# Two landing places and four split places in the weight ring of a six-layer fp32 kernel

## The chip, the cores and the metric

The kernel runs on one NeuronCore of a Trainium2 chip. The metric is the device time of one execution in microseconds (us), as the median of several runs. TensorE is called PE, VectorE DVE, ScalarE ACT, GpSimd POOL; SyncE (SP) issues nearly all DMAs.

## The reference, cut to what matters

A sequence of 256 tokens with 1024 channels goes through two blocks, everything in fp32. The first block has an RWKV-7 layer and a sparse attention layer (DSA), each with a SwiGLU layer behind it, and all four are modulated by vectors made from a condition `c`. The second has four residual layers: FoX attention, GLA, gated delta net (GDN), FoX attention.

```python
mod = silu(c) @ ada_w[i] + ada_b[i]            # 1024 x 6144, twice: one vector times a matrix
hin = x * (1 + sc1) + sh1
y = rwkv7(hin) or dsa_attention(hin)
x = layernorm(ALPHA * x + (1 + gt1) * y)
hin = x * (1 + sc2) + sh2
x = layernorm(ALPHA * x + (1 + gt2) * ((silu(gate) * up) @ ffn_w_out))
...
for layer in range(4):                         # fox, gla, gdn, fox
    x = x + mixer(rms_norm(x))                 # each: @ w_in, the mixer, @ w_out
```

Every weight matrix is used once, so some 240 MB of weights are streamed from HBM in one execution.

## The kernel before, in words

**Chunks.** `plan` cuts every weight matrix into chunks: KG = 4 row blocks of 128 rows by up to 512 columns, 1 MB when full. All chunks of the program stand in one list in the order in which they are used, numbered by `g`. There are 224: 48 *direct* ones, which belong to `ada_w`, and 176 others.

**Landing ring.** `w_raw` has NRAW places. Chunk `g` lands in place `g % NRAW`. SP issues the DMAs in the order of the list, and before it issues chunk `g` it waits until chunk `g - NRAW` has been consumed. A direct chunk is consumed when PE has multiplied it (L294, `Ada.pe_sums`: the condition vector times the chunk; an item is two chunks). Any other chunk is consumed when ACT has written its rounded part `w_hi` (L188, `split_hi`) and DVE has written the rest `w_lo` (L197, `split_lo`).

```python
if c["g"] >= NRAW:
    old = self.chunks[c["g"] - NRAW]
    sp.wait_ge(self.direct if old["direct"] else self.lo_done, old["idx"] + 1)
```

**Split ring.** `w_hi` and `w_lo` have NSPL places each. ACT and DVE wait with chunk `idx` until PE has used chunk `idx - NSPL`. PE makes an fp32 product of three passes, x_hi w_hi, x_hi w_lo and x_lo w_hi (L220 to L222, `mm_block`): 24 matmuls for a full chunk and 256 tokens.

**Stages.** The program is a row of stages; at each boundary all engines meet. A projection stage (`stage_project`, `stage_ffn_in`, `stage_rwkv_in`) runs over column blocks of two chunks each, and on each engine everything stands in one written order. `stage_project` writes it like this for ACT and for DVE:

```python
for m, c in enumerate(chunks):
    while due and c["idx"] - NSPL >= job[due[0]][-1]["idx"]:
        take(due.pop(0))
    if m >= done:
        split(c)
```

`take(n)` copies the finished block `n` out of PSUM and then does the side work of that block (`fox_sides`, `gla_sides`, `gdn_sides`, `bias_sides`). So with NSPL = 3 block `n` is taken after the split of chunk `2n+3` and before that of `2n+4`. In the FoX projection one piece of side work is `lf` on DVE (L2153, side work of block 2), and PE has two small matmuls that read it (L2159) behind its block 2, which is chunks 4 and 5.

**Start of a projection.** The activations are normalised, turned by PE (L535) and split too (`act_lead`, `dve_lead`). For the three projections behind a layernorm (both `ffn_in` and `dsa_in`) an `ada` item is put in there: PE multiplies it (L294), ACT copies it out (L312), PE turns it into a column (L302). ACT's order there is `split(0)`, then the `ada` copy, then the normalisation (`xn`, L517), and then the activations' high parts. PE's order is the item, ten filler matmuls (`keep_warm`, L204), the turn L302, four more fillers, the transposes L535.

**Ada elsewhere.** Items stand in `stage_begin` (four), `rwkv_lora` (two), `rwkv_prepare` (two), in `rwkv_mid` (six between pairs of small matmuls, L1287 and L1311, and two at the end), in `dsa_prepare` (one), `dsa_select` (three), `dsa_attend` (one).

Of the kernel before, what the change touches and what calls it, by code (L numbers as in the profile page):

```python
# [17 lines left out]
KD = D // P  # L18
COLS = 512
KG = 4  # L20
NRAW = 3
NSPL = 3
F = 2816
NEG = -1.0e30

# [47 lines left out]
class Core:  # L73

    def __init__(self, nc, a, ctx):
# [12 lines left out]
        self.modc = self.fixed("modc", [P, 2, 6 * KD])  # L89
        self.raw = self.fixed("w_raw", [P, NRAW, KG, COLS])  # L90
        self.s0 = self.at
        top = end // 32 * 32
        size = NSPL * KG * COLS * 4
        self.lo_at, self.hi_at = top - size, top - 2 * size
# [4 lines left out]
        self.ps = ctx.enter_context(nc.psum_tensor("ps", [P, 8, COLS], F32))  # L99
        self.wsem = [ctx.enter_context(nc.semaphore(f"w_landed{i}")) for i in range(NRAW)]  # L100
        self.hi_done = ctx.enter_context(nc.semaphore("w_hi_done"))
# [22 lines left out]
    def split_rings(self):  # L124
        return (self.place("w_hi", [P, NSPL, KG, COLS], self.hi_at, F32R),
                self.place("w_lo", [P, NSPL, KG, COLS], self.lo_at, F32R))

# [11 lines left out]
    def plan(self, name, w, blocks, direct=False):  # L139
# [3 lines left out]
        for cols in blocks:  # L143
# [3 lines left out]
            for k0 in range(0, ktot, KG):  # L147
                nk = min(KG, ktot - k0)
                g = len(self.chunks)
                kind = sum(c["direct"] == direct for c in self.chunks)  # L150
                self.chunks.append(dict(g=g, slot=g % NRAW, direct=direct, idx=kind, k0=k0, nk=nk,
                                        width=width, w=w, cols=cols))
# [8 lines left out]
    def issue(self, sp, upto):  # L161

        upto = min(upto, len(self.chunks))
        while self.issued < upto:
            c = self.chunks[self.issued]
# [3 lines that stand above are left out]
# [9 lines left out]
    def issue_mod(self, sp, items):  # L178
        l, b = items[-1]
        self.issue(sp, self.mod[l, b][-1]["g"] + 1 + NRAW)  # L180

    def split_hi(self, act, hi, c):

        s = c["idx"] % NSPL
        act.wait_ge(self.wsem[c["slot"]], self.landed(c))
        if c["idx"] >= NSPL:
            act.wait_ge(self.used, c["idx"] - NSPL + 1)  # L187
        self.nc.scalar.copy(hi[:, s, 0:c["nk"], 0:c["width"]],  # L188
# [3197 lines left out]
```

## Time and profile before

| what | value |
|---|---|
| median of 3 runs | 1651.54 us (1649.9 to 1652.76) |
| the profiled execution: its own time | 1648.74 us |
| the profiled execution: span of its instructions | 1647.0 us |
| PE busy | 1488.5 us, 90% of the span |
| DVE busy | 872.5 us, 53% |
| ACT busy | 670.2 us, 41% |
| DMA from the SP queue, share of 16 engines | 46.6% |
| mean DMA rate | 148 GB/s |

Busy time is the union of an engine's instructions. The instructions are in the order of the program, so the place of a row tells its stage: the begin stage ends at 39 us, `rwkv_mid` runs from 179 to 310, the three projections behind a layernorm start at 343, 563 and 755, the two FoX projections at 985 and 1487.

### The profile page before, as it was taken

The page shows a single profiled execution, that of the slowest core. Times are in us where ns is not written, and L with a number is a line of the kernel's source. Part 1 is how long each engine was busy: PE and PEld are TensorE (multiplying, and loading weights), DVE is VectorE, ACT ScalarE, POOL GpSimd, SP SyncE.
Part 4 walks back from the last instruction along what each step waited for, and adds up shares of the span by engine and source line. Part 5 has one row for each costly group of instructions (what it writes and reads, how often), then busy time and mean ns, then how long its engine had stood idle before and what let it go on. Part 6 is the DMA issues. An engine that isn't in the chain of part 4 may idle for free. (4 is left out here: it accounts for less than half of the span.)

```text
span 1647.0 us, 19055 instructions
## 1 busy us (share of the span) xinstructions
PE 1488.5 (90%) x7546; PEld 1171.5 (71%) x7546; DVE 872.5 (53%) x1161; ACT 670.2 (41%) x917; POOL 199.3 (12%) x109
## 2 busy tenths in 40 slices
PE   6999899989999998888999989978998985878987
PEld 2774669758877675565887868966886875767976
DVE  0756683764535454356554445745435587465644
ACT  1533432334333235343443316544452675235542
POOL 0005440130000110303000000300000032300300
PEclk8999899999999998899999989999999997899999
DMA  8655380546545564424653528814533531027821
GB/s 313 215 171 151 129 307 1 191 143 202 181 128 192 165 218 144 146 86 144 205 180 127 204 94 183 211 51 138 177 100 93 180 114 53 1 77 161 206 94 52
DMA packets 156852, 244.11 MB, mean 148 GB/s; under 512 B 14022, under 2 KB 95898, under 8 KB 156252
## 3 DMA queue, kind: packets, MB, share of 16 engines
q1 hardware_dynamic: 155612, 237.56, 46.6%
q0 software_dynamic: 1152, 5.34, 0.9%
q8 instruction: 60, 0.98, 0.3%
q14 instruction: 28, 0.23, 0.0%
HBM read 241.77 MB, written 1.11 MB: 147 GB/s over the span
## 5 line engine op out<-in xcount | busy, mean ns | idle before, releaser
L197 DVE TENSOR_TENSOR w_lo<-w_raw,w_hi 128x2048 fp32r<-128x2048 f32 (+3 forms) x176 | 393.0, 2240 | 291.8 <-ACT w_hi L188 291.6
L220 PE MATMUL ps<-w_hi,act_hi 128*128 128x512 f32 (+4 forms) x1216 | 470.4, 387 | 20.9 <-DVE act_lo L568 8.3
L188 ACT CAST w_hi<-w_raw 128x2048 fp32r<-128x2048 f32 (+3 forms) x176 | 316.2, 1802 | 380.0 <-PE ps L222 212.1
L222 PE MATMUL ps<-w_hi,act_lo 128*128 128x512 f32 (+4 forms) x1216 | 463.5, 381 | 0.0
L221 PE MATMUL ps<-w_lo,act_hi 128*128 128x512 f32 (+4 forms) x1216 | 463.1, 381 | 0.0
L220 PEld LDWEIGHTS ps<-w_hi,act_hi 128*128 128x128 f32 x1216 | 230.7, 190 | 68.3 <-DVE act_lo L568 12.0
L221 PEld LDWEIGHTS ps<-w_lo,act_hi 128*128 128x128 f32 x1216 | 230.6, 190 | 36.8 <-issue 1.2
L222 PEld LDWEIGHTS ps<-w_hi,act_lo 128*128 128x128 f32 x1216 | 230.5, 190 | 36.9
L204 PE MATMUL ps<-con 128*128 128x512 f32 x208 | 102.9, 640 | 24.3 <-DVE up L3165 18.0
L204 PEld LDWEIGHTS ps<-con 128*128 128x128 f32 x208 | 41.1, 209 | 70.7 <-issue 70.7
L294 PE MATMUL ps<-w_raw,condz 128*32 128x512 f32 x384 | 61.8, 748 | 23.7 <-DMA w_raw<-in_ada_w 13.7
L698 ACT ACTIVATE proj<-ps,nstat 128x456 f32<-128x456 f32 (+2 forms) x64 | 37.2, 632 | 105.3 <-PE ps L222 105.3
L220 PE MATMUL ps<-w_hi,ffn_gh 128*128 128x512 f32 x176 | 70.0, 398 | 0.0
L221 PE MATMUL ps<-w_lo,ffn_gh 128*128 128x512 f32 x176 | 69.6, 395 | 0.0
L222 PE MATMUL ps<-w_hi,ffn_gl 128*128 128x512 f32 x176 | 69.6, 395 | 0.0
L465 POOL TENSOR_TENSOR nstat<-nstat,con 128x2 f32<-128x2 f32 x7 | 4.9, 698 | 498.6 <-DVE nstat L487 299.4
L839 ACT ACTIVATE ffn_s<-ps 128x256 f32<-128x256 f32 x44 | 14.5, 381 | 93.8 <-PE ps L222 93.8
L294 PEld LDWEIGHTS ps<-w_raw,condz 128*32 128x32 f32 x384 | 10.4, 120 | 50.2 <-issue 25.8
L864 DVE TENSOR_TENSOR ffn_h<-ffn_s,ps 128x256 f32<-128x256 f32 x44 | 16.6, 418 | 53.4 <-PE ps L817 45.0
L302 PEld LDWEIGHTS ps<-con,ada_part 128*128 128x128 f32 x192 | 29.6, 234 | 21.3 <-issue 17.3
L312 ACT COPY ada_part<-ps 128x512 f32<-128x512 f32 x24 | 14.0, 583 | 66.7 <-PE ps L294 66.7
L220 PEld LDWEIGHTS ps<-w_hi,ffn_gh 128*128 128x128 f32 x176 | 33.1, 188 | 9.0 <-DVE w_lo L197 1.2
(479 smaller groups left out, 1834.5 us busy)
## 6 DMA issues: line engine op xcount, KB each, us to landing
w_raw<-in_ada_w SPq DMA_DIRECT2D x48, 1024.0 KB, 6.3
w_raw<-in_ffn_w_in SPq DMA_DIRECT2D x88, 512.0 KB, 4.9
w_raw<-in_fox_w_in SPq DMA_DIRECT2D x32, 912.0 KB, 8.8
w_raw<-in_ffn_w_out SPq DMA_DIRECT2D x20, 1024.0 KB, 5.1
w_raw<-in_rwkv_w_rkv SPq DMA_DIRECT2D x12, 1024.0 KB, 6.3
w_raw<-in_gla_w_in SPq DMA_DIRECT2D x10, 896.0 KB, 4.7
w_raw<-in_gdn_w_in SPq DMA_DIRECT2D x10, 896.0 KB, 4.9
w_raw<-in_fox_w_out SPq DMA_DIRECT2D x8, 1024.0 KB, 5.0
```

Source lines behind the costliest of these rows:

```text
L188: self.nc.scalar.copy(hi[:, s, 0:c["nk"], 0:c["width"]], self.raw[:, c["slot"], 0:c["nk"], 0:c["width"]]).then_inc(self.hi_done, 1)
L197: self.nc.vector.tensor_tensor(lo[:, s, 0:c["nk"], 0:c["width"]], self.raw[:, c["slot"], 0:c["nk"], 0:c["width"]], hi[:, s, 0:c["nk"], 0:c ...
L204: self.nc.tensor.matmul(self.ps[:, bank, :], self.c("ident"), moving, start=True, stop=True)
L220: nc.tensor.matmul(out(t)[:, 0:w], xh[:, k, tok], hi[:, s, j, 0:w], start=first, stop=False)
L221: nc.tensor.matmul(out(t)[:, 0:w], xh[:, k, tok], lo[:, s, j, 0:w], start=False, stop=False)
L222: r = nc.tensor.matmul(out(t)[:, 0:w], xl[:, k, tok], hi[:, s, j, 0:w], start=False, stop=last)
L294: r = core.nc.tensor.matmul(self.sums[32 * j:32 * j + 32, :], core.condz[:, k, :], core.raw[:, c["slot"], j, :], start=(k < KG), stop=(k > ...
L302: r = core.nc.tensor.matmul(self.turned[:, 4 * n + j:4 * n + j + 1], self.part[n % 2][:, j * P:j * P + P], core.c("ones")[:, 0:1], start=T ...
L312: core.nc.scalar.copy(self.part[n % 2][:, :], self.sums).then_inc(sem("ada_part"), 1)
L698: core.nc.scalar.activation(dst(n, t), out(t), ACT.Copy, scale=scale).then_inc(sem("taken"), 1)
L839: nc.scalar.activation(act_s[:, n % 2, t, :], ps[:, 2 * (n % 2) + t, 0:T], ACT.Silu).then_inc(sem("silu"), 1)
L864: nc.vector.tensor_tensor(h_s[:, n % 2, t, :], act_s[:, n % 2, t, :], ps[:, 2 * (n % 2) + t, T:2 * T], ALU.mult).then_inc(sem("h"), 1)
```

## The change

The landing ring gets two places in place of three, the split rings four places each in place of three. Nothing else is edited; but both constants are also used in the written orders: SP looks NRAW chunks ahead at the end of a stage, and `stage_project` and `stage_rwkv_in` place the taking of a block by NSPL. A place is 8 KB of each partition, and there are two split rings, so the rings grow from 72 to 80 KB and the scratch space between them shrinks by 8 KB.

```diff
 COLS = 512
 KG = 4
-NRAW = 3
-NSPL = 3
+NRAW = 2
+NSPL = 4
 F = 2816
```

## Rows read from the trace of the kernel before

**Rows 1.** Page, its head.
```profile
span 1647.0 us, 19055 instructions
```
**Rows 2.** Tile w_raw: durations ns min/median/max, and who waited for its users.
```profile
L188 ACT CAST w_hi<-w_raw x176: 862/1900/1943, 47.0 to 1624.9; 128x2048 fp32r<-128x2048 f32 x106, 128x1824 fp32r<-128x1824 f32 x36, 128x1792 fp32r<-128x1792 f32 x24, 128x1024 fp32r<-128x1024 f32 x4
L197 DVE TENSOR_TENSOR w_lo<-w_raw,w_hi x176: 992/2286/4490, 48.9 to 1626.9; 128x2048 fp32r<-128x2048 f32 x106, 128x1824 fp32r<-128x1824 f32 x36, 128x1792 fp32r<-128x1792 f32 x24, 128x1024 fp32r<-128x1024 f32 x4
...
  PEld ps L220: 1.2, 2
```
**Rows 3.** Waits of PE: who, for whom, us in total, times, longest.
```profile
PE ps L294 <- DMA w_raw<-in_ada_w: 13.7, 9, 3.8
PE ps L2691 <- ACT acc L2679: 12.3, 4, 4.7
```
**Rows 4.** Windows, eight chunks of the RWKV projection, users of w_hi: length, busy, clock, DMA.
```profile
57.90:101.42 43.52, 39.42 (x129) 24.03 (x128) 17.37 (x8) 15.29 (x8) 1.00 0.66 228
```
**Rows 5.** DMA issues at 208.16 and 209.01: count, KB, us to landing.
```profile
w_raw<-in_ada_w SPq DMA_DIRECT2D x1, 1024.0 KB, 5.2
...
w_raw<-in_ada_w SPq DMA_DIRECT2D x1, 1024.0 KB, 7.0
```
**Rows 6.** Timeline of ACT, GDN projection, casts ahead of a wait of PE.
```profile
1354.96 2.94 ACT L188 CAST w_hi<-w_raw 128x1600 fp32r<-128x1600 f32 x2
```
**Rows 7.** Timeline of PE, begin stage, its last ada chunk.
```profile
29.99 1.93 PE L294 MATMUL ps<-w_raw,condz 128*32 128x512 f32 x8 [0.67 <-DMA w_raw<-in_ada_w]
```
**Rows 8.** Timeline of PE, rwkv_prepare, its last ada chunk.
```profile
176.27 1.07 PE L294 MATMUL ps<-w_raw,condz 128*32 128x512 f32 x8 [0.75 <-DMA w_raw<-in_ada_w]
```
**Rows 9.** Timeline of PE, rwkv_mid: second, sixth and last ada item.
```profile
213.39 1.06 PE L294 MATMUL ps<-w_raw,condz 128*32 128x512 f32 x8 [0.44 <-DMA w_raw<-in_ada_w]
...
236.59 1.92 PE L294 MATMUL ps<-w_raw,condz 128*32 128x512 f32 x16
...
305.06 1.06 PE L294 MATMUL ps<-w_raw,condz 128*32 128x512 f32 x8 [1.77 <-DMA w_raw<-in_ada_w]
```
**Rows 10.** Timeline of PE, dsa_select, its last ada item.
```profile
659.90 3.69 PE L294 MATMUL ps<-w_raw,condz 128*32 128x512 f32 x16
```
**Rows 11.** DMA issues at 344.7, 564.7 and 756.9.
```profile
w_raw<-in_ffn_w_in SPq DMA_DIRECT2D x1, 512.0 KB, 7.9
...
w_raw<-in_dsa_w_in SPq DMA_DIRECT2D x1, 1024.0 KB, 7.0
...
w_raw<-in_ffn_w_in SPq DMA_DIRECT2D x1, 512.0 KB, 7.6
```
**Rows 12.** Timeline of ACT, then of PE, start of the first ffn_in.
```profile
343.14 1.90 ACT L188 CAST w_hi<-w_raw 128x2048 fp32r<-128x2048 f32 x1 [13.23 <-PEq L236]
345.79 0.58 ACT L312 COPY ada_part<-ps 128x512 f32<-128x512 f32 x1 [0.76 <-PE ps L294]
...
351.01 0.95 PE L302 MATMUL ps<-con,ada_part 128*128 128x1 f32 x8
...
353.62 1.91 PE L535 MATMUL ps<-con,xn 128*128 128x128 f32 x16
```
**Rows 13.** DMA issues at 988.6, 992.2 and 1010.8: FoX chunks 3, 4 and 8.
```profile
w_raw<-in_fox_w_in SPq DMA_DIRECT2D x1, 912.0 KB, 5.4
...
w_raw<-in_fox_w_in SPq DMA_DIRECT2D x1, 912.0 KB, 9.1
...
w_raw<-in_fox_w_in SPq DMA_DIRECT2D x1, 912.0 KB, 8.4
```
**Rows 14.** Timeline of DVE, then of PE, first FoX projection.
```profile
1016.52 4.03 DVE L197 TENSOR_TENSOR w_lo<-w_raw,w_hi 128x1824 fp32r<-128x1824 f32 x2 [5.00 <-ACT w_hi L188]
1020.47 0.17 DVE L2153 TENSOR_TENSOR lf<-tmp 128x16 f32<-128x16 f32 x1
...
1020.79 0.60 PE L2159 MATMUL ps<-ntri,lf 128*8 128x256 f32 x2
```
**Rows 15.** Windows, behind a wait of PE of 18 us that ends at 1405.8.
```profile
1405.80:1409.20 3.40, 3.40 (x4) 1.46 (x5) 3.37 (x2) 0.00 (x0) 0.00 (x0) 0.51 0.00 0
```

## The prediction, made before the changed kernel was run

> **What bounds the kernel now.** I read the head of the page, then the waits of PE, then everything that touches w_raw, then the timelines where the two views pointed. PE is busy for 90% of a span of 1647.0 us [rows 1]. It never waits for a landed or a split weight in a projection: the only such wait in 176 chunks is 1.2 us, of the weight load [rows 2]. Where it does wait for landings is the ada work, nine times, 13.7 us in all [rows 3]. So the reader is to see two uses of one landing ring. In projections it has slack: eight chunks take PE 43.5 us, 5.44 each, at full clock [rows 4], while a place is free again after landing (5.2 us alone [rows 5]), cast 1.9 and subtraction 2.3 [rows 2], 9.4 us; three places give a chunk each 3.1 us, two give one each 4.7 us. In ada work PE eats a chunk in 1.1 us, and only what has landed ahead hides a landing.
>
> **What the edit moves.** (a) SP issues a chunk when the chunk two before is consumed, no longer three before. (b) ACT and DVE may split four chunks ahead. (c) In the written order, take(n) and its side work move behind the split of chunk 2n+4. (d) The addresses of the scratch tiles shift; no row prices that, I put it at 0 (a large effect would have to be in every stage alike).
>
> **Fourth split place: what it can bring.** PE's wait for splits is 1.2 us, so (b) alone can give back at most that. By (c) casts run before side work instead of after it. PE waits for ACT four times in the GDN projection, 12.3 us [rows 3]; ahead of one of them ACT has two casts of 2.94 us together [rows 6], of which one can now be done earlier, half of it: -1.3 with the subtraction it frees. The other three have no cast in front. I take -1.3; the ends are 0 and -13.5.
>
> **Ordinary projections.** 4.7 us for a chunk against PE's 5.44, and four split chunks as a cushion: cost 0. The cover is 0.75 us a chunk; it is gone when landings take over 6.6 us.
>
> **Ada streams.** Two chunks issued 0.86 us apart land after 5.2 and 7.0 us, so at 213.3 and 216.0, 2.7 apart [rows 5]; in a queue each further chunk costs 2.7, and the latency of an empty queue shows in full at 5.1 to 5.2.
> Begin: the chunks 2 to 7 are each issued one consumption later. Chunk 6 goes out behind x, lands at 29.7, and chunk 7, issued when 5 is eaten at 26.2, lands 2.7 behind it at 32.4; before, PE began it at 29.99 [rows 7]. +2.4.
> rwkv_prepare: its two items are four chunks. The third is issued at 171.1 and lands 176.2, the fourth 2.7 later, where PE began at 176.27 [rows 8]. +2.7.
> rwkv_mid: the pair at 207.0 has landed early in both kernels. The next pair is issued at 208.2 and 209.0 and lands at 213.3 and 216.0: its second chunk is done at 217.1, not at 214.45 (213.39 + 1.06 [rows 9]). From there each first chunk lands 5.1 us behind the end of the first one before it, each second chunk 5.1 behind the second before it but at least 2.7 behind its partner, and PE has 4.0 us of small matmuls between: pairs end at 217.1, 223.4, 231.1, 237.4, 245.1. The last of these ended at 238.5 [rows 9]: +6.6, and PE is what the stage goes by here, its next step is fixed filler. At the end two items stand in a row: third chunk issued when the first is eaten, lands 5.1 later, the fourth 2.7 behind: begin of the last at 314.35 in place of 305.06 + 6.6 [rows 9], +2.7. DVE's last work ended 0.6 us behind PE's before, which hides 0.6 of it. +8.7 for the stage.
> dsa_select: six chunks, two landed ahead instead of three. Chunks 3 to 6 land at 656.2, 658.9, 663.2, 666.0; the last item ended at 659.90 + 3.69 = 663.6 [rows 10], now at 668.0. The topk on DVE is done by then and filler follows on PE. +4.4.
> rwkv_lora, dsa_prepare, dsa_attend: at most two chunks are wanted before a pause longer than 8 us. 0. Together 18.2. Bounds: 9 (every chunk beyond the first late one hidden by a clock that is at half level anyway), 25.
>
> **Start of the three projections behind a layernorm.** This is the wait that I look for first, because it blocks something else. The list has ada, ada, chunk 0. With three places chunk 0 is issued when the last chunk of the stage before is split, long ahead. With two, both places hold the ada chunks, and chunk 0 is issued when PE has eaten the first, at 344.2, 564.7 and 756.3, behind the loads of the layernorm's gains. The chunks issued at these moments before landed at 352.6, 571.7 and 764.3 [rows 11] (their second halves, issued 0.4 to 0.6 later). ACT begins its stage with split(0), where it stood at 343.14 [rows 12]: it now stands idle until 352.6, casts 1.9, copies the ada part 0.6 [rows 12], and PE turns it at 355.1 instead of 351.01. Behind the turn come fillers and the transposes 2.6 us after it, at 357.8, where they stood at 353.62 [rows 12]: +4.2. Queued behind ACT's cast is also the normalisation, which PE's transposes need; it is done at 357.4, just in time. The same sum for the others gives +3.8 (transposes at 573.20 before) and +5.5 (764.09 before). Together 13.5. Bounds: 5, if PE's idle fillers could be passed; 17, if POOL's work on x, which moves too, slows more of DVE's.
>
> **The two FoX projections.** Here landings are slower: 5.4 us for chunk 3, 9.1 for chunk 4, 8.4 for chunk 8 [rows 13], each issued with at most one other chunk still on its way. Chunks 2, 4, 6, 8 share one place. A chunk is cast in 1.7 (1.9 scaled to 456 columns) and subtracted in 2.0 [rows 14], with handovers 3.85. So: 2 is issued when chunk 0 is split, 988.6, lands 994.0; 4 is issued 997.9, lands 1007.0; 6 is issued 1010.9, lands 1016.1 (5.2 taken); 8 is issued 1020.0, lands 1028.4, split at 1032.3. PE is hardly late yet (chunk 5 is split at 1016.7, needed at 1015.7). But lf stood on DVE right behind the split of chunk 7 and was ready at 1020.6, just as PE came to use it at 1020.79 [rows 14]. By (c) it now stands behind the split of chunk 8: ready at 1032.4. PE waits in front of L2159: +11.7. While it waits, the ring fills, so the later slow chunks cost nothing more. The second FoX layer has the same pattern 501.8 us on: together +23.4. Lower bound: all landings 5.4, then 8 is split at 1025.8, +5.2 each. Upper bound: 14 each, with the slow chunks afterwards uncovered. After a wait of 18 us PE ran 3.4 us at a granted clock of 0.51 [rows 15], that is at the level of 1.2 GHz, half its work lost: 1.7 for each of these two waits, 3.4.
>
> The Trainium skill bears on (a). "Trainium Kernel Development and Optimization", Best Practices, says "Double-buffer for performance: Overlap DMA with compute". That a second buffer is enough would make (a) free, and the sum would be -1.3; the trace agrees for the ordinary projections (4.7 against 5.44) and speaks against it wherever something else than a steady stream waits. [...]
>
> **The sum.** 18.2 + 13.5 + 23.4 + 3.4 - 1.3 = 57.2 us. The profiled execution took 1648.74 (span 1647.0, 1.7 around it), 2.8 below the median, so I add to the median: 1651.5 + 57.2 = 1709.
>
> **Rivals.**
> 1. FoX landings were slow only through company, and two places make each 5.4. For it: 5.4 for chunk 3. Against: chunk 8 had none. Waits of 5.2 each and no lost clock: 1651.5 + 18.2 + 13.5 + 10.4 - 1.3 = 1692.
> 2. The starts are covered: chunk 0 lands early enough, or fillers absorb the delay. For it: SP's queue is short there. Against: fillers are in order, nothing can pass them. 57.2 - 13.5: 1695.
> 3. Landings overlap more often than I think and take 7.0 us [rows 5] everywhere: a place turns in 11.3, a chunk each 5.65 against 5.44. 0.2 for some 140 chunks, 29 more: 1738. Against: one chunk in flight, while the other is split.
> 4. Two landing places are enough, as the skill's rule has it, and PE finds its work: -1.3 to 0, 1650 to 1652. This is also the case that the edit does nothing. Against: ada work waits even with three.
> 5. Faster: side work with ACT and DVE no longer behind casts. All four waits in GDN and the 1.2 go, -13.5: 1638. It decides if the landing terms stay under 13.5 in sum. For it: 12.3 us in rows 3. Against: three of the four waits have no cast in front.
>
> **Numbers.** Forecast 0.57, rival 1 0.13, rival 2 0.10, rival 3 0.12, rival 4 0.05, rival 5 0.03. The range 1685 to 1730 takes in the forecast with its bounds and rivals 1 and 2, and leaves out 0.2. A measurement of this kernel can tell 0.2%, 3.3 us, from no change. Faster 0.03, within it 0.05, slower 0.92.
>
> **What would show it.** In the profile after: PE's waits for w_raw<-in_ada_w near 30 us instead of 13.7; L188 at the start of both ffn_in and of dsa_in waiting for a DMA, with L535 behind it 4 to 5.5 us late; in front of L2159 a wait of some 10 us for DVE's L2153, twice, with L197 before it waiting for a cast that waits for in_fox_w_in; and in ffn_out, gla_in and the plain projections no wait for w_lo. It would be wrong if chunks were issued earlier than the list says, if FoX landings shrink, or if a wait in the steady stream shows up at L220.

## The result: 79.5 us slower, 4.9%

The changed kernel takes 1730.2 us (median of 4 runs, 1725.1 to 1740.2), the kernel before 1650.7 (4 runs, 1647.3 to 1652.8); the ratio is 1.0491, 95% interval 1.0434 to 1.0549. Run once more beside other kernels it gave 1734.0 (6 runs, 1724.9 to 1743.3) and a ratio of 1.0500 (1.0466 to 1.0534). The prediction was 1709, range 1685 to 1730: the direction is right, the loss is 1.4 times the forecast one, 79.5 us for 57.2, and the time just outside the range. The execution profiled took 1734.73 us, 86.0 above that of before, so the readings below add up to 86.0.

The page of the changed kernel, its head and the row of the granted clock in 40 slices of the span (9 is 90% or more of full speed):

```profile
span 1733.0 us, 19054 instructions
PEclk9999779898999999799999999899999997989999
```

The two 7s side by side are the slices from 173 to 260 us, rwkv_prepare and rwkv_mid. The waits of PE, in us, times and longest, as in [rows 3]:

```profile
PE ps L294 <- DMA w_raw<-in_ada_w: 33.6, 21, 4.5
PE ps L2159 <- DVE lf L2153: 22.8, 2, 11.6
PE ps L302 <- ACT ada_part L312: 13.3, 5, 5.0
PE ps L2691 <- ACT acc L2679: 10.9, 4, 3.5
PE ps L220 <- DVE w_lo L197: 0.6, 1, 0.6
```

Against [rows 3] the waits for ada landings have grown from 13.7 to 33.6 us, there is a wait for lf of 11.6 and one about as long, and the turn of the ada sums now waits for ScalarE. The steady stream is as it was: one wait of 0.6 us for a split weight, and in this window over the RWKV projection, all of PE's instructions counted and not only the users of w_hi as in [rows 4], PE is busy from end to end at full clock (in the kernel before it is 43.52 of 43.52 us too):

```profile
57.90:101.42 43.52, 43.52 (x194) 36.05 (x193) 28.88 (x28) 22.71 (x19) 0.00 (x0) 1.00 0.66 233
```

I laid the two traces side by side, chunk by chunk, and took by how much later PE begins each chunk. What each stretch adds, with the forecast behind it:

| stretch | added, us | forecast |
|---|---|---|
| begin | 3.5 | 2.4 |
| rwkv_prepare | 4.5 | 2.7 |
| rwkv_mid | 25.6 | 8.7 |
| dsa_select and its neighbours | 4.7 | 4.4 |
| starts of ffn_in0, dsa_in, ffn_in1 | 7.0, 4.7, 7.0 | 4.2, 3.8, 5.5 |
| FoX projections | 14.4, 14.5 | 13.4 each (11.7 wait, 1.7 clock) |
| GDN and all the rest | 0.1 | -1.3 |
| sum | 86.0 | 57.2 |

So one row is off by 17 us and the others by 3 at most. (The 0.1 is a sum of small terms of both signs, +1.3 in the first ffn_out and -0.7 from GDN to the next FoX layer among them.) The row that is off, rwkv_mid, in the profile, as windows that hold the same work of PE: from the first ada item of rwkv_mid to the sixth, and from there to the next item. Columns: window, its length, busy us and instructions of PE, PEld, DVE, ACT and POOL, granted clock, DMA share, GB/s. First the kernel before:

```profile
207.00:238.51 31.51, 30.74 (x250) 18.88 (x249) 29.28 (x66) 11.52 (x21) 12.71 (x12) 1.00 0.94 329
238.51:298.79 60.28, 60.28 (x580) 56.18 (x580) 25.34 (x44) 13.51 (x22) 10.02 (x4) 1.00 0.11 38
```

Then the changed kernel, with a third window inside the first:

```profile
214.90:264.75 49.85, 41.64 (x250) 25.17 (x249) 31.37 (x67) 11.72 (x21) 14.85 (x13) 0.76 0.67 224
264.75:328.37 63.62, 63.62 (x582) 58.20 (x581) 22.12 (x42) 13.53 (x22) 7.32 (x3) 0.95 0.07 24
225.75:233.08 7.33, 7.33 (x32) 6.37 (x32) 6.81 (x16) 1.76 (x3) 1.34 (x2) 0.50 0.62 225
```

The same 250 matmuls keep PE busy for 41.64 us instead of 30.74. Of the 18.3 us that this window grew, 7.4 are idle time and 10.9 are slower work. The third window shows what kind: PE never stands in it, has no ada chunk in it, and runs at a granted clock of 0.50, the level of 1.2 GHz. About as many bytes come in over a longer time, at 224 GB/s for 329. The first two windows once more, now cut where the granted clock changes:

```profile
214.90:221.66 6.76, 5.33 (x45) 3.15 (x48) 6.14 (x19) 2.73 (x5) 1.30 (x2) 1.00 0.66 229
221.67:235.31 13.64, 12.65 (x60) 7.24 (x56) 12.64 (x30) 2.83 (x5) 3.44 (x3) 0.50 0.56 195
235.32:245.55 10.23, 6.90 (x57) 3.96 (x49) 9.62 (x19) 1.66 (x3) 2.65 (x3) 1.00 0.87 288
245.56:255.79 10.23, 10.23 (x48) 6.88 (x48) 2.94 (x2) 2.83 (x5) 1.27 (x2) 0.50 0.38 123
255.80:266.03 10.23, 7.77 (x64) 5.21 (x61) 0.00 (x0) 2.25 (x4) 7.45 (x4) 1.00 0.96 309
266.04:272.86 6.82, 6.82 (x19) 4.40 (x19) 0.00 (x0) 1.07 (x2) 2.76 (x1) 0.50 0.44 154
272.87:328.37 55.50, 55.50 (x553) 52.51 (x551) 22.12 (x42) 11.87 (x19) 3.26 (x2) 1.00 0.00 1
```

The level alternates with the items. PE stands in every second one (2.4, 3.3 and 2.5 us in all). Soon behind each of these waits the clock falls to half; while PE works at half clock the next two chunks land, so that the item between has no wait, and the clock comes back. In PE's timeline the first wait stands just before the window from 225.75 to 233.08, and the lines behind L1311 are later waits of the stage:

```profile
221.25 1.58 PE L294 MATMUL ps<-w_raw,condz 128*32 128x512 f32 x8 [1.43 <-DMA w_raw<-in_ada_w]
223.81 1.93 PE L294 MATMUL ps<-w_raw,condz 128*32 128x512 f32 x8 [0.99 <-DMA w_raw<-in_ada_w]
...
229.48 3.67 PE L1311 MATMUL ps<-v,kgram 128*128 128x64 f32 x16
...
244.46 1.06 PE L294 MATMUL ps<-w_raw,condz 128*32 128x512 f32 x8 [2.94 <-DMA w_raw<-in_ada_w]
...
334.81 1.93 PE L294 MATMUL ps<-w_raw,condz 128*32 128x512 f32 x8 [3.53 <-DMA w_raw<-in_ada_w]
337.52 1.93 PE L294 MATMUL ps<-w_raw,condz 128*32 128x512 f32 x8 [0.78 <-DMA w_raw<-in_ada_w]
```

PE stands 1.43 and 0.99 us; the ada chunk behind the second takes 1.93 us (1.06 in [rows 9]), and the matmuls of L1311 take 3.67 (2.00 in the kernel before). The start of ffn_in0, which answers to [rows 12], first ACT, then PE:

```profile
385.94 1.90 ACT L188 CAST w_hi<-w_raw 128x2048 fp32r<-128x2048 f32 x1 [22.20 <-DMA w_raw<-in_ffn_w_in]
387.74 0.58 ACT L312 COPY ada_part<-ps 128x512 f32<-128x512 f32 x1
...
388.38 1.87 PE L302 MATMUL ps<-con,ada_part 128*128 128x1 f32 x8 [5.02 <-ACT ada_part L312]
393.66 2.93 PE L535 MATMUL ps<-con,xn 128*128 128x128 f32 x16
```

ACT stands at its first cast for a landing, the copy of the ada sums queues behind it, PE waits 5.02 us, and then the turn (L302) and the transposes (L535) run at the lower clock, 1.87 and 2.93 us where [rows 12] have 0.95 and 1.91. And the first FoX projection, DVE and PE, for [rows 14]:

```profile
1089.25 2.06 DVE L197 TENSOR_TENSOR w_lo<-w_raw,w_hi 128x1824 fp32r<-128x1824 f32 x1 [4.42 <-ACT w_hi L188]
1091.23 0.17 DVE L2153 TENSOR_TENSOR lf<-tmp 128x16 f32<-128x16 f32 x1
...
1091.45 1.02 PE L2159 MATMUL ps<-ntri,lf 128*8 128x256 f32 x2 [11.58 <-DVE lf L2153]
```

This is the forecast chain: lf behind the split of a late chunk. PE began the projection 58.1 us late, and the forecast had lf ready at 1032.4 on the old scale, so at 1090.5; it was ready at 1091.4.

### The profile page after: what moved, and what is told of

Same layout as the page of the kernel before. It is cut to its first block and busy times, and to the rows that moved or that the text cites. A ratio compares the mean times of both kernels' runs of the same rounds, so it can differ in the third digit from the quotient of the medians.

```text
span 1733.0 us, 19054 instructions
## 1 busy us (share of the span) xinstructions
PE 1524.2 (88%) x7546; PEld 1189.1 (69%) x7546; DVE 867.7 (50%) x1161; ACT 669.8 (39%) x917; POOL 194.2 (11%) x109
## 5 line engine op out<-in xcount | busy, mean ns | idle before, releaser
L197 DVE TENSOR_TENSOR w_lo<-w_raw,w_hi 128x2048 fp32r<-128x2048 f32 (+3 forms) x176 | 386.7, 2208 | 294.9 <-ACT w_hi L188 294.8
L204 PE MATMUL ps<-con 128*128 128x512 f32 x208 | 113.8, 697 | 24.5 <-DVE up L3165 18.3
L294 PE MATMUL ps<-w_raw,condz 128*32 128x512 f32 x384 | 69.8, 832 | 42.4 <-DMA w_raw<-in_ada_w 33.6
L204 PEld LDWEIGHTS ps<-con 128*128 128x128 f32 x208 | 45.0, 229 | 75.5 <-issue 75.5
L839 ACT ACTIVATE ffn_s<-ps 128x256 f32<-128x256 f32 x44 | 14.5, 382 | 133.0 <-PE ps L222 133.0
L302 PEld LDWEIGHTS ps<-con,ada_part 128*128 128x128 f32 x192 | 35.4, 277 | 37.9 <-ACT ada_part L312 19.2
L302 PE MATMUL ps<-con,ada_part 128*128 128x1 f32 x192 | 36.7, 314 | 13.4 <-ACT ada_part L312 13.3
```

The costliest lines, as they stand in the source:

```text
L197: self.nc.vector.tensor_tensor(lo[:, s, 0:c["nk"], 0:c["width"]], self.raw[:, c["slot"], 0:c["nk"], 0:c["width"]], hi[:, s, 0:c["nk"], 0:c ...
L204: self.nc.tensor.matmul(self.ps[:, bank, :], self.c("ident"), moving, start=True, stop=True)
L294: r = core.nc.tensor.matmul(self.sums[32 * j:32 * j + 32, :], core.condz[:, k, :], core.raw[:, c["slot"], j, :], start=(k < KG), stop=(k > ...
L302: r = core.nc.tensor.matmul(self.turned[:, 4 * n + j:4 * n + j + 1], self.part[n % 2][:, j * P:j * P + P], core.c("ones")[:, 0:1], start=T ...
L839: nc.scalar.activation(act_s[:, n % 2, t, :], ps[:, 2 * (n % 2) + t, 0:T], ACT.Silu).then_inc(sem("silu"), 1)
```

## The experiments

"Ring" below is the ring of landing places. Every time stands beside the kernel before on the same chip (1649.4 to 1652.1); the ratio has its 95% interval.

**1. Landing places alone: three split places kept.**

```diff
-NRAW = 3
+NRAW = 2
```

> Two landing places, three split ones: the half of the change that takes away. Against the kernel before. Theory (landing place is the whole loss): the ada waits on PE stay near 33 us, the layernorm leads and rwkv_mid as in the changed kernel; in the FoX projections lf is cast one chunk earlier in the written order, so each of the two long waits (11.6 and 11.3 us) shrinks by 2 to 4 us; GDN's two casts wait again for a place (its wait about 4.7, not 3.3 us). Sum: within 8 us of the changed kernel's 1730, about 1725. Rival (the fourth split place and the order that goes with it make a large part of the loss): the FoX waits vanish, under 1710. Rival (the fourth place softens the loss): over 1738.

Measured: 1729.3, ratio 1.0481 (1.0446 to 1.0516). The landing place alone gives practically the whole loss in time. Its waits of PE for lf and for ACT in GDN:

```profile
PE ps L2691 <- ACT acc L2679: 12.3, 4, 4.7
PE ps L2159 <- DVE lf L2153: 8.2, 2, 4.6
```

GDN's wait is that of before, as expected. Each lf wait shrank by some 7 us, more than the 2 to 4 that I gave it. The FoX projections add 7.5 and 8.3 us, not 14.4 and 14.5. These 13 us less are in the profiled execution, which at 1719.95 us is the fastest of the four; the median is only 1 us below that of the changed kernel, so the medians don't show them.

**2. The changed kernel with the written order as for three split places.**

```diff
-                while due and c["idx"] - NSPL >= job[due[0]][-1]["idx"]:
+                while due and c["idx"] - 3 >= job[due[0]][-1]["idx"]:
```

(and the same in the written order of the RWKV projection)

> The changed kernel (2 landing, 4 split) with the written order of the evacuations and side work as it was for three split places. Theory as predicted (order alone makes the FoX wait, since lf was ready before): the two waits of PE for lf go from 11.6 and 11.3 us to 1 or less, 1705 us. Rival (lf waits for landings of chunks ahead of it in either order, the order adds only one chunk of it): the waits shrink to 7 to 9 us each, 1722 to 1726. In both cases the ada waits and GDN are unchanged.

Measured: 1726.1, ratio 1.0462 (1.0437 to 1.0486), PE's wait for ACT in GDN again 12.3 us, the two FoX projections +7.7 and +10.6. The theory (1705, waits of 1 us) is refuted and the rival has the time, but not its waits of 7 to 9 us: they are 7.7 us for both together. The order is some 4 to 7 us of each projection's 14, the landings are the rest. With the wait for lf shorter, PE comes to the late chunks sooner: it now waits 4.7 us for their split parts (`w_lo`), for 0.6 in the changed kernel. GDN's gain is gone although the fourth split place is there, so it takes the place and the order together.

**3. The order alone: the kernel before with the written order as for four** (the edit of experiment 2, with 4 in place of NSPL = 3).

> The kernel before (3 landing, 3 split) with the written order as it would be for four split places, and nothing else. Theory (the order costs only where a late landing stands ahead of it): with three landing places lf is 3 to 5 us later than PE wants it, twice: 1655 to 1660 us. Rival (order alone makes the 11 us waits): 1674. Rival (order costs nothing with three landing places): 1650.7, no different.

Measured: 1665.9, ratio 1.0104 (1.0081 to 1.0128), and these waits:

```profile
PE ps L2691 <- ACT acc L2679: 13.5, 4, 4.4
PE ps L2159 <- DVE lf L2153: 8.1, 2, 4.0
```

The lf waits are as expected, but the time is 6 us above the expected 1655 to 1660. With the lower clock behind them the projections add 6.4 and 7.0 us. Added to the 7.5 and 8.3 of the first run that is 13.9 and 15.3, near the 14.4 and 14.5 of both together. Of the rest, 3.1 us lie in GDN; of 5.9 us that the profiled execution is late before ffn_in0, 4.9 are gone again before FoX, and I can assign neither. In the times the halves don't add: 79.7 us for the landing place alone and 16.3 for the order alone are 96, for the 79.5 of both. So only the FoX terms can be added, and the order costs less where the landings are late already.

**4. Don't let PE stand for lf.** L2159 moves from behind block 2 to behind block 4 of the FoX projections, then to behind block 3, then to block 3 with the pool engine's second root ahead of the gate's transfers in its queue.

```diff
-    @on("pe", 2)
+    @on("pe", 4)
     def _(pe, sem):
         pe.wait_ge(sem("lf"), 1)
```

> The changed kernel with PE's two small matmuls on lf put behind block 4 of each FoX projection rather than behind block 2, so that PE doesn't stand still for lf; nothing else. If the long waits are the cost of FoX (11.6 and 11.3 us, and 1.2 us of lower clock behind each) and nothing else is late behind them: 25 us less than the changed kernel, 1705 us. Rival (PE stands still because chunks land too slowly and would wait for weights in its place): 2 to 8 us less, 1722 to 1728.

> The changed kernel with PE's matmuls on lf behind block 3 of each FoX projection (block 2 in the kernel, block 4 in the last such run, where PE then stood 5.8 us twice waiting for the normalized q and k that the pool engine makes behind ncum). Theory (what was saved at lf there was given back at the norm, since the pool's queue holds ncum ahead of the second norm): with one block less delay the wait for lf is 2 us or less and the norm's wait 0 to 2 us, so each projection gains 9 to 12 us and the time is 1708 to 1714. Rival (with two landing places PE waits for weights instead): 1722 or more.

> The changed kernel with PE's matmuls on lf behind block 3, and in the pool engine's queue the second reciprocal root (for the norm) ahead of the gate's transfers (ncum out and in) rather than behind them. Theory (FoX's loss is a chain of small steps whose order was tight for three landing places: lf first, then the norm): both the lf wait and the 5.4 us norm waits vanish and each FoX projection is 0 to 4 us longer than in the kernel before (14.4 us in the changed kernel): 22 to 27 us less than the changed kernel. Rival (two landing places hold the projection however the side work is ordered): 8 to 12 us less, as with the matmul moved alone.

Measured: 1733.5 (1.0503, 1.0465 to 1.0540), 1724.5 (1.0456, 1.0400 to 1.0513) and 1728.1 (1.0466, 1.0442 to 1.0491; the changed kernel beside it 1734.0). The gains that I expected, 25, 16 to 22 and 22 to 27 us, failed all three times; only in the second did the rival hold. Each wait for lf shrank to 1.2 us or less, and the projections still add 10 and 7 us in the third. There, first DVE and then PE:

```profile
1118.52 2.06 DVE L197 TENSOR_TENSOR w_lo<-w_raw,w_hi 128x1824 fp32r<-128x1824 f32 x1 [5.51 <-ACT w_hi L188]
1120.50 2.29 DVE L2218 TENSOR_TENSOR proj<-proj,st 128x2048 f32<-128x2048 f32 x1
...
1122.84 2.40 PE L2231 MATMUL ps<-con,proj 128*128 128x128 f32 x10 [4.01 <-DVE proj L2218]
```

It is the same picture one step on: the norm now stands behind a split that waits 5.51 us for a late chunk, and PE waits for the norm. The pool's queue was not the main cause: with it reordered PE still waits 6.5 us for the norm, 9.7 without, and the times of the two runs don't differ clearly. Every small step of this projection is written between splits, so with two landing places the whole chain of steps is late.

**5. The ada streams alone, with two landing places; everything else with three.** (A second line, not shown, makes SP stop one chunk earlier where the last chunk that it looks ahead to is an ada chunk.)

```diff
+            if c["direct"] and c["g"] >= 2:
+                old = self.chunks[c["g"] - 2]
+                sp.wait_ge(self.direct if old["direct"] else self.lo_done, old["idx"] + 1)
```

> The kernel before (3 landing, 3 split, its written order), but an ada chunk's transfer also waits until the chunk two before it is used, so that the ada streams alone run as with two landing places and the projections with three. Theory (the streams with an unsplit chunk on PE are where most of the loss is, through landing and then through the lower clock): PE's waits for ada landings 30 us or more, rwkv_mid 20 to 28 us longer, the sum over the five ada stages 32 to 45 us: 1683 to 1695 us. Forecast of the prediction for the same streams: 18.2 us, 1669. Rival (the loss in rwkv_mid comes from the projection's chunks or from the moved buffers): under 1660.

Measured: 1688.0, ratio 1.0229 (1.0197 to 1.0261), +38.6 us. The table above has 38.3 for these streams, the forecast 18.2. (The execution profiled here was the fastest of four, 34.9 us above that of before.) The waits are nearly those of the changed kernel:

```profile
PE ps L299 <- DMA w_raw<-in_ada_w: 34.4, 21, 4.4
```

**6. rwkv_mid alone with two landing places** (chunks 16 to 31 of the 48, held as in experiment 5), **and the same with extra matmuls** ahead of the second chunk of each item but the first; their results go nowhere.

```diff
         for c in core.mod[l, b]:
+            for _ in range(warm if c["k0"] else 0):
+                core.nc.tensor.matmul(core.ps[:, 7, 256:512], core.c("ident"), core.con[:, 0:256], start=True, stop=True)
             pe.wait_ge(core.wsem[c["slot"]], core.landed(c))
```

> The kernel before, with only the ada chunks used in rwkv_mid (16 of 48) held to two landing places; every other chunk has three. The prediction gave this stage +8.7 us; the profiles of the changed kernel show its end some 25 to 30 us later than before. Theory (the stage's stream alone loses 18 to 25 us): 1669 to 1675 us. Rival (the prediction's size was right and the rest comes from neighbouring stages): 1658 to 1661.

> The same, with six extra matmuls of 256 columns ahead of the second chunk of each ada item but the first in rwkv_mid, so that TensorE's granted clock stays up. Theory (about 10 us of this stage's loss is the halved clock on the small matmuls between the chunks): 6 to 10 us less than the run without them. Rival (the landings alone set the stage's pace, so the slower matmuls lie in time that would be waited anyway, or the extra matmuls cost what they give): within 3 us.

> As the run with six extra matmuls, with four (1.7 us at full clock). With six the granted clock stayed up, but PE then had work without a pause between the chunks (3.79 us from one chunk to the next and 4.97 to the item behind, 8.76 an item), so the filler itself set the pace and the stage was still 16 us longer than before. Four fit in the 1.6 to 1.7 us by which a chunk lands behind its partner. Theory (clock and landings share the loss, and the prediction's sum of +8.7 holds for a stream at full clock): 1659 to 1663 us, an item near 7.5 us. Rival (the clock falls again with less filler): 1672 or more.

> The same with two extra matmuls (0.87 us). Theory: the pauses that are left, near 0.8 us each, either leave the clock up, and the time is that of four extra matmuls or 1 us less, or they bring half clock back in part: 1665 to 1672. Without extra matmuls it was 1678.8.

Measured, with the stage's length from the first ada matmul to the end of the last one (before 99.1 us, from 207.0 to 306.1; changed kernel 124.6):

| extra matmuls | time | ratio (95%) | stage |
|---|---|---|---|
| none | 1678.8 | 1.0166 (1.0142 to 1.0191) | 125.6 |
| two | 1666.4 | 1.0094 (1.0065 to 1.0122) | 114.6 |
| four | 1663.8 | 1.0077 (1.0050 to 1.0104) | 112.7 |
| six | 1667.0 | 1.0100 (1.0076 to 1.0125) | 119.4 |

The stage's stream alone costs 28.5 us, more than the 19 to 25 expected. Giving PE more to do takes 12 to 15 us off the kernel's time, where 6 to 10 had been expected of six; four miss their 1659 to 1663 by 1 us, two are within theirs. Each stage length is of one execution: in the ten others that have two landing places here and no extra matmul it is 120.1 to 128.7 us, in the three others with six it is 117.6 to 119.7. Windows over the same work, none first, then four:

```profile
205.69:255.60 49.91, 42.30 (x250) 24.91 (x249) 31.54 (x67) 11.72 (x21) 15.07 (x13) 0.74 0.68 227
255.60:319.96 64.36, 64.36 (x582) 59.28 (x581) 22.13 (x42) 13.51 (x22) 7.01 (x3) 0.94 0.07 21
```

```profile
210.46:252.40 41.94, 40.47 (x290) 25.90 (x289) 31.57 (x67) 11.51 (x21) 14.60 (x12) 1.00 0.78 261
252.40:312.68 60.28, 60.28 (x580) 56.17 (x580) 22.14 (x42) 13.50 (x22) 7.93 (x4) 1.00 0.08 29
```

With 40 instructions more (20 matmuls, each recorded as two), PE is busy for less time, 40.47 us for 42.30, at a clock of 1.00 for 0.74. The second window has no extra matmul in it and still falls from 64.36 to 60.28, exactly the length it has before the change. Six are worse than four since they take more than the pause: an ada chunk follows its partner's start after 3.79 us with six, 2.92 with four. The first late item still has its pause with four, and the clock stays at 1.00 behind it:

```profile
216.85 1.06 PE L301 MATMUL ps<-w_raw,condz 128*32 128x512 f32 x8 [1.47 <-DMA w_raw<-in_ada_w]
```

**7. The extra matmuls (six) in the changed kernel,** run twice:

> The changed kernel, with six matmuls of 256 columns (about 2.6 us at full clock, their output unused) ahead of the second chunk of each ada item but the first in rwkv_mid. Theory (PE's waits pull the granted clock to half, and the small matmuls between the ada chunks then take 7.3 us instead of 4.0): the granted clock of rwkv_mid near 1.0, the pair's matmuls 1.06 us a chunk, the stage 8 to 14 us shorter although PE has more to do: 1717 to 1723 us. Rival (the clock is low for another reason, or the stage is held by landings alone): no shorter, 1730 to 1742.

> The changed kernel with the extra matmuls in rwkv_mid a second time. In its first run the ada matmuls of rwkv_mid all took 0.59 us (full clock) and the end of the stage came 26.4 us late, against 29 to 39 us for the six others, but the median of its times was not below the changed kernel's. Theory (the lower clock is worth 8 to 10 us in rwkv_mid): beside the changed kernel on the same chip 6 to 12 us less. Rival (the extra matmuls cost as much as the clock gives back): within 3 us of it.

Measured: 1734.0 (1.0501, 1.0466 to 1.0537) and 1732.6 (1.0486, 1.0464 to 1.0508), the latter beside the changed kernel's 1734.0. The clock came back and the stage fell to 117.6 and 119.7 us, but the medians hardly moved. The unaltered changed kernel, profiled once more beside the second, had a stage of 122.3, so that only 2.6 us of it are a gain over its neighbour. On these runs alone the rival stood; it is why experiment 6 was made.

**8. The first split behind the normalization,** in the changed kernel and in the kernel before.

```diff
-        split(0)
         if self.ada:
             self.ada.act_part(act, sem, 0)
         self.act_norm(act, sem)
+        split(0)
```

> The changed kernel with ScalarE's cast of the projection's first chunk put behind ada_part and the normalization in the lead of each projection with an ada item, so that the late landing of that chunk no longer holds ada_part. Theory of the prediction (leads +13.5 us because the cast stands ahead): the waits of the turn matmuls for ada_part fall from 13.3 us to 4 or less, ffn_in0, dsa_in and ffn_in1 each 4 to 7 us shorter: 1712 to 1718 us. Rival (the chunk is as late for the first block as it was for ada_part): the waits move to the first block's w_lo, 1726 to 1732.

> The kernel before with the cast of each projection's first chunk behind ada_part and the normalization in the lead. With three landing places that chunk has landed in time in most leads, so nothing is waited for there: within 3 us of 1650 us. Rival (some of the 7 to 11 us that the leads wait for the turn of the ada sums comes from this cast): 4 us or more faster.

Measured: 1718.0, ratio 1.0416 (1.0375 to 1.0456), some 12 us less than the changed kernel; in the kernel before 1651.5, ratio 0.9999 (0.9981 to 1.0017), no different. PE's waits for ada_part in front of the turn (L302) fall from 13.3 to 1.4 us; a part comes back as the first block's wait for its operand `act_lo` (L576), 11.7 us for 6.2. The starts of the three projections fall from 7.0, 4.7 and 7.0 to 3.4, -0.2 and 3.3 us.

**9. Both repairs together, then with six extra matmuls.**

> The changed kernel with both repairs of written order: first split behind the normalization, lf matmul behind block 3 with the second root ahead of the gate's transfers. Each alone gave about 13 us and 6 us. Theory (they lie at different places, so they add): 1711 to 1716 us, still 60 us above before, since the ada streams are untouched. Rival (the landing ring takes back at the next place what one repair saves): 1718 or more.

> The same with the extra matmuls in rwkv_mid. Theory of the clock: 6 to 10 us less than the run without them, 1703 to 1709. Rival: within 3 us of it.

Measured: 1709.5 (1.0354, 1.0327 to 1.0380) and 1704.1 (1.0321, 1.0297 to 1.0344). The repairs add up: 22.6 us by the ratios, 1 to 2 us more than expected. The extra matmuls gain 5.4 us here, at the edge of the expected 6 to 10. More than 50 us of the loss stay; no version was found that beats the kernel before.

## Why the prediction fell short, step by step

**What bounds the kernel; ordinary projections at 0.** Right: 0.6 us of waits for split weights in 176 chunks. Rival 3, landings of 7.0 everywhere, is near in time (1738), but the loss in the steady stream that makes it did not come.

**Ada streams, 18.2 us: this is the step that failed.** It measured 38.6 us alone (experiment 5). In the prediction's words, each second chunk lands "at least 2.7 behind its partner, and PE has 4.0 us of small matmuls between". The landings do come so: PE begins the two chunks at 221.25 and 223.81, as they land; the forecast's 213.3 and 216.0, with the 7.9 us by which the stage's first item is late, are 221.2 and 223.9. But the 4.0 us are a duration at full clock. PE now stands 2.4 to 3.3 us in every second item, the granted clock falls to 0.50 behind it, and the small matmuls take 7.3 us, the chunks 1.93 for 1.06. From 217.1 on the forecast let the pairs end 6.3, 7.7, 6.3 and 7.7 us after one another; they end 10.3, 9.4, 10.7 and 8.6 apart, and it is the pairs without a wait that are 4 us longer. The forecast even named half clock, as the reason for its lower bound, and priced it for the FoX waits only. The run with four extra matmuls divides the stage's 26.5 us (125.6 against 99.1): 12.9 are gone with the clock back up, and the 13.6 that stay are landings plus what the extra matmuls themselves take, for a forecast of 8.7. In the times it is 28.5 and 11.8 us. This divides single executions, and the stage differs by several us between executions (experiment 6). The same mechanism is a part of rwkv_prepare, whose last chunk took 1.93 us for the 1.07 of [rows 8].

"TensorE: Matmul & The Clock Gate" of the Trainium skill, section HAM oscillation — how this bites in real kernels, describes a loop in which waits for transfers between batches of matmuls bring the lower clock back each time. Its waits are longer, about 3 to 5 us. The trace agrees in part: 0.50 behind waits of 1.43 and 0.99, of 2.94 and of 2.46 us, but a clock of 1.00 behind one of 1.47 in experiment 6. I hadn't weighed that section against this change.

**Starts behind a layernorm, 13.5 us.** Mechanism right: ACT's cast waited for the landing, and taking it out of the way gave back some 12 us. The size was 18.7. What was missing is again the clock behind each wait, in ffn_in0 0.9 us on the turn, 1.8 on the four fillers behind it (3.76 us for 1.96) and 1.0 on the transposes, and in ffn_in0 and ffn_in1 waits of 5.0 and 4.9 us where 4.2 and 5.5 had been forecast as the whole.

**FoX, 23.4 and 3.4 us.** Place, mechanism and size right: waits of 11.6 and 11.3, 1.2 and more for the clock behind each, 28.9 in all against 26.8. Chunks 4, 6 and 8 took 9.3, 5.7 and 8.7 us to land, for 9.1, 5.2 and 8.4 in the forecast. Over the 32 chunks of 912 KB of the two FoX projections the median time to landing did shrink, which rival 1 supposed and the prediction named as a sign that it is wrong (page of the kernel before, then of the changed kernel):

```profile
w_raw<-in_fox_w_in SPq DMA_DIRECT2D x32, 912.0 KB, 8.8
...
w_raw<-in_fox_w_in SPq DMA_DIRECT2D x32, 912.0 KB, 6.0
```

Chunks 4 and 8, on which the wait for lf rests, stayed slow, and that is in part luck: why some chunks land in 5.5 us and others in 9 isn't shown. Rival 1's objection that chunk 8 had no company isn't quite right: chunk 7 was still on its way for the first 0.9 us.

What the prediction laid at the door of the order ("By (c) it now stands behind the split of chunk 8") is only half of it: with the old order and two landing places the projections still add 7.5 to 10.6, and with the new order and three places 6.4 and 7.0. And the wait is not a single one: moved off L2159, it returns at the norm.

**GDN, -1.3.** PE's wait fell from 12.3 to 10.9, as forecast. It needs the fourth split place and the later order together (experiments 2 and 3). From the start of GDN's projection to that of the next FoX, PE gains 0.7 us.

**The rivals.** The second, covered starts, and the first, FoX landings of 5.4 us, are refuted by the waits above, though the first is right that most FoX landings shrink. The fourth, two places are enough ("Double-buffer for performance", Best Practices in "Trainium Kernel Development and Optimization" of the Trainium skill), holds for the projections outside FoX and for nothing else here. The fifth, faster, had 1.4 us to show for its 13.5.

**What stays open.** The same kernel varies more with two landing places (1724.9 to 1743.3 in 6 runs) than with three (1646.7 to 1659.7 in 17), and its slower runs have the lower mean clock (0.929 and 0.937 at the two ends); what tips an execution wasn't found. Nor is it shown why six extra matmuls gave 12 us with rwkv_mid alone changed, 5 with the repairs and 1 in the changed kernel as it is.

## What to carry to other kernels

A ring's depth is tested where the consumer is fast, not where it is busiest on average: here PE waited 0.6 us in all for the split parts of 176 chunks with some 5 us of work each, and 48 others, with 1.1 us of work each, cost 38 us. When you price a short wait of TensorE, price the work behind it too, at half clock: look in the windows for the granted clock behind waits of the same length, and for work that PE shares between two waits. And before you move an operation off a late step, follow the whole chain written into the same queues: the next step is behind the same transfer.

## What the runs showed of the hardware that I had not expected

In the changed kernel PE ran at a granted clock of 1.00 until it had stood for 1.43 us; the clock was 0.50 from 0.4 us into the next work on, for 13.6 us (221.67 to 235.31) in which PE stood only once, for 0.99 us. The length of a pause alone doesn't decide it: 1.47 us at the same place in the run with four extra matmuls, and 1.27 us in rwkv_mid of experiment 5, were followed by 1.00. What does decide isn't shown.

The lower clock can begin after the work has resumed: the wait of 2.46 us ended at 263.69, the clock was 1.00 to 266.03 and 0.50 to 272.86. These 6.8 us are all the halved work in the window of 63.62 us at a mean of 0.95, and they make it 3.3 us longer than the 60.28 of before.

Extra work of some 1.9 us in each item (2.92 from chunk to chunk, less 1.06 for the chunk) kept the clock at 1.00 and made the stage 12.9 us shorter, the whole kernel 15.
